# ScalarE, not VectorE, scales the attention probabilities of a three-block fp32 network

## The reference, cut to what matters

```python
s = jnp.where(mask, s, -jnp.inf)
m = jnp.max(s, axis=-1, keepdims=True)
e = jnp.where(mask, jnp.exp(s - m), 0.0)
den = jnp.sum(e, axis=-1, keepdims=True)
p = e / jnp.maximum(den, 1e-30)
o = jnp.einsum("bqgrk,bqkgd->bqgrd", p, v)
...
return gb[..., 0:1] * o_c + gb[..., 1:2] * o_s + gb[..., 2:3] * o_w
```

## Time and profile before

| | us |
|---|---|
| median of three timed runs | 1673.26 |
| lowest, highest | 1668.85, 1673.39 |
| time of the profiled execution | 1669.05 |
| its span, first to last instruction | 1667.3 |
| TensorE busy in the span | 1584.3 (95%) |
| VectorE, ScalarE, GpSimd busy | 795.2, 634.7, 564.6 |
| mean granted TensorE clock | 0.978 |

### The profile page before, as it was taken

One profiled execution on the slowest core, in us unless ns is written; L12 is line 12 of the kernel. 1 busy time (PEld: TensorE's weight loads), 2 busy tenths in 40 slices (PEclk: granted clock), 3 DMA queues, 4 the chain that ended last, 5 costly groups with the idle time before them and its releaser, 6 DMA issues.

```text
span 1667.3 us, 20477 instructions
## 1 busy us (share of the span) xinstructions
PE 1584.3 (95%) x7110; PEld 1215.1 (73%) x7110; DVE 795.2 (48%) x1417; ACT 634.7 (38%) x1126; POOL 564.6 (34%) x236
## 2 busy tenths in 40 slices
PE   7999899999999987789999999999989999999997
PEld 5666678888888866456878888888767766666685
DVE  6863432223444677684342223444655345455434
ACT  4343332223223465555432232232533434544432
POOL 4221244444444333100444444444235421121241
PEclk9999999999999988999999999999989999999998
DMA  5111123323323221100222223232123311111121
GB/s 214 61 59 39 63 89 101 96 93 101 100 89 101 80 84 64 38 1 1 87 91 91 98 93 102 96 101 94 58 88 114 114 64 39 38 51 38 41 86 51
DMA packets 36624, 129.55 MB, mean 78 GB/s; under 512 B 4048, under 2 KB 4176, under 8 KB 36560
## 3 DMA queue, kind: packets, MB, share of 16 engines
q1 hardware_dynamic: 35136, 124.80, 22.5%
q10 hardware_dynamic: 1424, 3.90, 0.6%
HBM read 126.58 MB, written 2.10 MB: 77 GB/s over the span
## 4 chain that ended last, share of the span: by engine, by line
issue 54%; PE 25%; POOL 20%; ACT 1%; DVE 1%; POOLq 1%; DVEq 0%; ACTq 0%
POOL w L558 20%; PE bank L575 5%; PE bank L577 5%; PE bank L576 5%; PE bank L681 3%; PE bank L708 3%; PE bank L690 2%; PE bank L935 0%; DVE arena L1975 0%; POOLq L557 0%; POOLq L555 0%; ACT arena L1367 0%; PE bank L906 0%; PE bank L644 0%; PE bank L870 0%
## 5 line engine op out<-in xcount | busy, mean ns | idle before, releaser
L558 POOL TENSOR_TENSOR w<-raw,w 128x1024 fp32r<-128x1024 f32 x232 | 564.4, 2435 | 1068.9 <-ACT w L1037 686.3
L575 PE MATMUL bank<-opC,w 128*128 128x512 f32 x624 | 259.2, 415 | 18.6 <-DVE opC L1435 10.3
L577 PE MATMUL bank<-opC,w 128*128 128x512 f32 x624 | 247.5, 397 | 0.0
L576 PE MATMUL bank<-opC,w 128*128 128x512 f32 x624 | 246.8, 396 | 0.0
L1578 DVE TENSOR_TENSOR mlp_op<-arena,mlp_op 128x512 fp32r<-128x512 f32 x64 | 144.4, 2259 | 188.7 <-ACT mlp_op L1153 188.7
L575 PE MATMUL bank<-mlp_op,w 128*128 128x512 f32 x560 | 221.8, 396 | 10.0 <-DVE arena L1498 9.5
L1125 ACT ACTIVATE w<-raw 128x1024 fp32r<-128x1024 f32 x126 | 133.2, 1057 | 239.4 <-PE bank L577 239.4
L576 PE MATMUL bank<-mlp_op,w 128*128 128x512 f32 x560 | 220.4, 393 | 0.0
L577 PE MATMUL bank<-mlp_op,w 128*128 128x512 f32 x560 | 220.2, 393 | 0.0
L575 PE MATMUL bank<-opA,w 128*128 128x512 f32 x428 | 168.7, 394 | 6.5 <-ACT arena L1301 2.6
L576 PE MATMUL bank<-opA,w 128*128 128x512 f32 x428 | 167.1, 390 | 0.0
(11 more groups left out here) (213 smaller groups left out, 2146.2 us busy)
## 6 DMA issues: line engine op xcount, KB each, us to landing
raw<-stream_dram SPq DMA_DIRECT2D x232, 512.0 KB, 3.4
out_t_dram<-arena SPq DMA_DIRECT2D x8, 256.0 KB, 2.2
x<-x_t_dram SPq DMA_DIRECT2D x4, 256.0 KB, 5.5
x<-x_t_dram ACTq DMA_DIRECT2D x4, 256.0 KB, 7.3
rope<-ropes_dram ACTq DMA_DIRECT2D x2, 512.0 KB, 6.7
con<-consts_dram ACTq DMA_DIRECT2D x1, 993.5 KB, 7.8
arena<-p_t_dram ACTq DMA_DIRECT2D x1, 512.0 KB, 4.1
par<-params_dram ACTq DMA_DIRECT2D x1, 253.5 KB, 3.7
```

The costliest lines, as they stand in the source:

```text
L558: pool.tensor_tensor(w_lo[:, j, :], raw[:, j, :], w_hi[:, j, :].bitcast(F32), ALU.subtract).then_inc(lo_made, 1)
L575: pe.matmul(out, wh, hi, start=first, stop=False)
L576: pe.matmul(out, wh, lo, start=False, stop=False)
L577: return pe.matmul(out, wl, hi, start=False, stop=last)
```

## The change

ScalarE scales unit s-2 at step s, right behind the exp of unit s and ahead of `between(s)` (where `prepare` stands) and of the copy of unit s-3. VectorE only makes the factor: the reciprocal, and for gated units a 128x1 product of reciprocal and gate, both now ahead of the mask of unit s. A new semaphore, share_made, hands the factor over.

```diff
@@ ScalarE, attention @@
                                              bias=negm[:, step:step + 1], scale=-1.0,
                                              accum_out=den[:, step:step + 1]).then_inc(exp_done, 1)
+                    i = step - NORM_LAG
+                    if 0 <= i < n:
+                        act.wait_ge(share_made, u0 + i + 1)
+                        pr = probs(i, units[i]["n"])
+                        nc.scalar.activation(pr, pr, ACT.Copy, scale=rden[:, i:i + 1]).then_inc(p_ready, 1)
                     between(step)
@@ VectorE, attention @@
                     i = s - NORM_LAG
                     if 0 <= i < n:
                         dve.wait_ge(exp_done, u0 + i + 1)
-                        inverted = mark(nc.vector.reciprocal(rden[:, i:i + 1], den[:, i:i + 1]))
+                        if units[i]["gate"] is None:
+                            nc.vector.reciprocal(rden[:, i:i + 1], den[:, i:i + 1]).then_inc(share_made, 1)
+                        else:
+                            step(nc.vector.reciprocal(rden[:, i:i + 1], den[:, i:i + 1]))
+                            TS(rden[:, i:i + 1], rden[:, i:i + 1], units[i]["gate"], None, ALU.mult).then_inc(share_made, 1)
...
-                    if 0 <= i < n:
-                        u = units[i]
-                        dve.wait_ge(vstep, inverted)
-                        pr = probs(i, u["n"])
-                        if u["gate"] is None:
-                            TS(pr, pr, rden[:, i:i + 1], None, ALU.mult).then_inc(p_ready, 1)
-                        else:
-                            TS(pr, pr, rden[:, i:i + 1], u["gate"], ALU.mult, ALU.mult).then_inc(p_ready, 1)
                     behind(s)
```

More of the change, by code:

```diff
@@ L333, in program @@
         bank = [ctx.enter_context(nc.psum_tensor(f"bank{i}", [P, SEQ], F32)) for i in range(8)]
+        share_made = sem("share_made")
         raw_in = [sem(f"raw_in{i}") for i in range(RING)]
```

## The result

| us | before | changed |
|---|---|---|
| median of 12 timed runs each, alternating on one chip | 1668.95 | 1673.91 |
| lowest, highest | 1667.82, 1673.5 | 1672.78, 1678.24 |
| profiled execution | 1669.05 | 1672.78 |
| span | 1667.3 | 1671.0 |
| VectorE, ScalarE busy | 795.2, 634.7 | 735.1, 701.4 |

The ratio is 1.0025, 95% interval 1.0014 to 1.0036. The changed kernel is slower by 0.25%, some 4.2 us: just inside the 0.3% that a measurement of this kernel can tell. The runs of the kernel before lie mostly in two groups, around 1668.5 (eight of twelve) and around 1673.4 (four); the median of the first three runs, 1673.26, came from the upper one. No execution of the upper group was profiled, so what makes its 4.9 us is not shown.

The account below looks back on a forecast made before the run. TensorE was taken to bound the kernel, with cost only where it waits on ScalarE's order: 2.6 + 1.1 + 1.5 + 0.9 = 6.1 us on 1673.3 gave 1679.4 us, range 1673 to 1686.

Parts of the forecast that it names:

- The base: Time before the change: median 1673.3 us, 4.2 above the profiled execution; the terms' 6.1 us were added to it.
- Six Silu in last: TensorE stalls before transposes for a scaling behind ScalarE's six Silu: 1.5 us, 3.6 or nearer 0.5 depending on the clock.
- The ring: mla steps 9 to 13: scaling enters the ScalarE-VectorE loop between exp and copy four times; 2.6 us, between 1.3 and 2.9.
- The end of mla: With no scores left, exp, copy and scaling take ScalarE 1.82 us a unit against TensorE's 1.60; 1.1 us, between 0.5 and 2.
- The two Silu: In last, transposes at 1460.74 wait for a 128x256 scaling behind the exp; 0.9 us, from 0 to 1.
- Start of mla: One scaling leaves VectorE's chain ahead of a 2.8 us wait, one enters ScalarE's; counted as nothing, -0.4 to +0.4.
- "even": First attention family: its 32 added scalings lie in ScalarE's idle time, as transposes come two steps later; no cost.
- Within 0.3%: Rival: ScalarE's idle time swallows more, terms at lower values sum to 3.2 us, 1676.5 us; chance 0.33.
- The clock rival: New idle time in mla's loop or the longer stall brings low-clock stretches, some 3.3 us each: 1682.7 or 1686; chance 0.16.
- VectorE's relief: Rival: shorter VectorE chain removes TensorE's three mask waits in mla, 4.2 us, giving 1669.1 us; chance 0.06.

Follow-up runs that it names:

- the doubled kernel: Changed kernel, with ScalarE in mla also copying each unscaled unit to a spare buffer ahead of its scaling; 1682.57 us, ratio 1.0083 to the kernel before.
- mla alone: Kernel before, with ScalarE doing the scalings of the mla family only; 1672.46 us, ratio 1.0024 to the kernel before.
- even alone: Kernel before, with ScalarE doing the scalings of the even family only; 1668.89 us, ratio 0.9999 to the kernel before.
- Silu units: Changed kernel, with the scalings of units 46 and 58 of last back on VectorE; 1672.57 us, ratio 1.0021 to the kernel before.
- eleven units on VectorE: Changed kernel, with mla units 7 to 10 and 27 to 31 and last units 46 and 58 scaled by VectorE; 1670.78 us, ratio 1.0011 to before.
- unit 46 alone: Kernel before, with only the scaling of unit 46 of last moved to ScalarE; 1669.06 us, ratio 1.0004 to the kernel before.
- the last one: Changed kernel, with every scaling ahead of the exp and that of last unit 46 on VectorE; 1669.75 us, ratio 1.0003 to the kernel before.

## Why the prediction was wrong in the number and right in the cause

**The base.** The step of the prediction that failed first is "I carry the same difference to it: 1673.3 + 6.1". I had one median of three runs that lay in two groups, and added the sum to the upper one. With 12 runs of each the kernel before takes 1668.95. That is 4.3 of the 5.5 us between 1679.4 and 1673.91. Against the profiled execution, the same sum gave 1675.2 where 1672.78 came, and added to 1668.95 it would have given 1675.1.

**The sum.** 6.1 us were forecast; 4.2 came by the ratio, 5.0 by the medians, 3.7 between the profiled executions. The step that failed here is the term "Six Silu in last", 1.5 us at the full clock. The stall came as described, 5.58 us, but the low clock came with it, and its net is 0.1 in the changed kernel, 0.2 with that scaling alone, 0.8 at most. I had named this case ("if more of the low stretch falls into the idle time, it is nearer 0.5") and taken the other value; rows of before said how much there was to win, since TensorE worked in all 6.50 us of the low-clock row. This term makes 1.4 of the 1.5 us between my 6.1 and the 4.7 that its places measured. That these 4.7 lie so near the profiled difference of 3.7 is in part luck: 1.6 us behind "last", which I had not foreseen, stood against some 2.6 us of small drifts the other way, the largest at the loading.

**What held.** The ring: 2.5 us for 2.6, with exps 3.85 to 3.89 apart for 3.9, and down to 0.5 with the four scalings put back. The end of mla: 1.0 for 1.1. The two Silu: 0.9 for 0.9. Start of mla +0.1 for 0. "even" -0.2 for 0. The profile after has its new waits where the text said they would be; the busy times moved by 67 and 60 us and not by 85.

**Slips in the working.** The end of mla comes to 1.0 by its own numbers (787.83 + 3.2 is 791.0, against 790.01). A fifth of 0.45 taken from "slower" leaves 0.52 and 0.42 for "same", not 0.54 and 0.4. One and a half low stretches on top of 1679.4 give 1684.4, not 1686. None of these bears on the result.

**The rivals.** "Within 0.3%" at 0.33 is what came, 4.2 us by the ratio, yet not by its mechanism in mla: there nothing more than forecast was swallowed; only its six Silu came true. The clock rival had its stretch once, 3.4 us behind "last" at a cost of 1.6, in a place with an unchanged stall, and in the doubled kernel inside the ring, where I had placed it, without a loss beyond the copies' own. VectorE's relief is visible at the start of mla (the longest wait went from 2.8 to 2.0 us), and the new wait for a scaling took it back in the same place. Nothing got faster.

## What to carry to other kernels

Work moved to an engine that is half idle is paid where that engine stands in a ring or at the head of a drain: find those places, and put the moved instruction into the idle time ahead of the wait, not behind it. Here the same 160 instructions cost 4.2 us behind the exp and nothing measurable ahead of it. And take the base of a forecast from many runs, or give the forecast as a difference: three runs of a kernel whose times lie in two groups say little about its median.

## What the runs showed of the hardware

- A longer stall can be nearly free if the low clock comes with it. At the six Silu 6.8 us at 1.2 GHz were spent in each of before, the changed kernel and the kernel with one scaling moved; what differed was how much of it was idle, 0.5, 3.6 and 3.5 us. 1.5 us more of stall came to 0.1 and 0.2.
- The same idle time need not have the same fall behind it. Behind "last" TensorE idles 2.17 us in every kernel I looked at. The clock fell behind it in the changed kernel and in four variants, and did not in before and six variants (mla alone, even alone, Silu units or eleven units on VectorE, unit 46 alone, and the last one). Its cost is 1.6 us. The five with the fall are just those in which ScalarE scales both unit 46 and unit 58 of "last", but these stand over 100 us ahead, and with one profile of each kernel I can't say what decides it, nor whether it comes in every execution.
- A scaling of 128x512 on ScalarE takes 0.70 to 0.72 us and its queue 0.61 to 0.63; one of 128x1 on VectorE takes 0.214 us.
